# Dilated heads interleaved with matrix tiles, and the layer embedding's projection placed after the output projection

## The reference

```python
# second block, in outline
h  = rmsnorm(x, g_mix) @ w_in          # 6 parts of 512 columns: b, c, x for the convolution; q, k, v
conv = b * causal_dwconv3(c * x)       # 512 wide
att  = dilated_attention(rmsnorm(q), rmsnorm(k), v)    # 8 heads of 64, causal, additive distance bias
x = x + concat(rmsnorm(conv), rmsnorm(att)) @ w_out
x = x + (silu(causal_dwconv3(rmsnorm(x) @ w_gate)) * (rmsnorm(x) @ w_up)) @ w_down     # 2816 wide
out = x + sigmoid(rmsnorm(x) @ w_ple_gate) * (p @ w_ple_proj)   # p: layer embedding, 512 x 256
```

## Time and profile before

| | us |
|---|---|
| median of 3 runs (lowest, highest) | 1833.47 (1832.82, 1835.03) |
| the profiled execution | 1833.88 |
| its span in the profile | 1832.0 |
| TensorE busy | 1790.5 |
| VectorE busy | 985.4 |
| ScalarE busy | 667.1 |
| GpSimd busy | 1.9 |

### The profile page before, as it was taken

How to read it: one execution, slowest core, us unless ns; L and a number is a source line. 1 busy time by engine, 2 the same in 40 slices (tenths; PEclk the granted TensorE clock), 3 DMA queues, 4 the chain that set the end, 5 groups by cost and what they waited for, 6 DMA issues and landing times.

```text
span 1832.0 us, 23458 instructions
## 1 busy us (share of the span) xinstructions
PE 1790.5 (98%) x9636; PEld 1527.6 (83%) x9636; DVE 985.4 (54%) x1423; ACT 667.1 (36%) x935; POOL 1.9 (0%) x11
## 2 busy tenths in 40 slices
PE   9999999999999999999999999989999999999998
PEld 7777998888889988988888889878878788888886
DVE  3666753434347576743434357646457665256554
ACT  3455441313133666432322236225344322122332
POOL 0000000000000000000000000000000000000000
PEclk9999999999999999999999999988889999999999
DMA  7220232232223112222222231210202223322341
GB/s 280 93 69 29 94 109 98 87 114 92 92 92 111 63 59 78 85 92 81 103 92 93 90 115 70 92 69 11 82 24 104 92 92 115 138 92 92 115 147 60
DMA packets 28596, 169.73 MB, mean 93 GB/s; under 512 B 2848, under 2 KB 7392, under 8 KB 9440
## 3 DMA queue, kind: packets, MB, share of 16 engines
q1 hardware_dynamic: 22592, 156.44, 23.9%
q10 hardware_dynamic: 5920, 12.08, 2.0%
HBM read 166.39 MB, written 5.27 MB: 94 GB/s over the span
## 4 chain that ended last, share of the span: by engine, by line
PE 89%; DVE 5%; ACT 3%; DMA 1%; issue 1%; DVEq 0%; SPq 0%; ACTq 0%
PE ps L1546 29%; PE ps L1548 28%; PE ps L1547 28%; PE ps L1679 2%; DVE w_lo L840 1%; ACT w_hi L407 1%; DMA stage<-slabs 1%; PE ps L1658 1%; PE ps L1892 0%; PE ps L1619 0%; ACT y L564 0%; PE ps L2024 0%; ACT act_hi L569 0%; PE ps L2034 0%; PE ps L1799 0%
## 5 line engine op out<-in xcount | busy, mean ns | idle before, releaser
L1546 PE MATMUL ps<-act_hi,w_lo 128*128 128x512 f32 (+1 forms) x1504 | 544.3, 362 | 8.1 <-DVE act_lo L840 2.6
L1548 PE MATMUL ps<-act_lo,w_hi 128*128 128x512 f32 (+1 forms) x1504 | 538.5, 358 | 0.0
L1547 PE MATMUL ps<-act_hi,w_hi 128*128 128x512 f32 (+1 forms) x1504 | 538.3, 358 | 0.0
L407 ACT ACTIVATE w_hi<-stage 128x2048 fp32r<-128x2048 f32 (+4 forms) x147 | 267.5, 1820 | 390.8 <-PE ps L1548 389.5
L840 DVE TENSOR_TENSOR w_lo<-stage,w_hi 128x2048 fp32r<-128x2048 f32 (+6 forms) x152 | 322.5, 2123 | 93.4 <-ACT w_hi L407 86.4
L1546 PEld LDWEIGHTS ps<-act_hi,w_lo 128*128 128x128 f32 x1504 | 284.2, 189 | 54.0 <-issue 5.9
L1548 PEld LDWEIGHTS ps<-act_lo,w_hi 128*128 128x128 f32 x1504 | 283.9, 189 | 42.0
L1547 PEld LDWEIGHTS ps<-act_hi,w_hi 128*128 128x128 f32 x1504 | 283.9, 189 | 40.2
L1546 PE MATMUL ps<-hid_hi,w_lo 128*128 128x512 f32 (+1 forms) x608 | 218.5, 359 | 2.1 <-DVE w_lo L840 2.1
L1548 PE MATMUL ps<-hid_lo,w_hi 128*128 128x512 f32 (+1 forms) x608 | 216.9, 357 | 0.0
L1547 PE MATMUL ps<-hid_hi,w_hi 128*128 128x512 f32 (+1 forms) x608 | 215.4, 354 | 0.0
(11 more groups left out here) (288 smaller groups left out, 2217.6 us busy)
## 6 DMA issues: line engine op xcount, KB each, us to landing
stage<-slabs SPq DMA_DIRECT2D x147, 1024.0 KB, 4.8
bias_rows<-bias_line ACTq DMA_DIRECT2D x1, 3072.0 KB, 16.3
strips<-dilated ACTq DMA_DIRECT2D x2, 1024.0 KB, 4.9
out<-y ACTq DMA_DIRECT2D x4, 512.0 KB, 2.6
y<-x_t ACTq DMA_DIRECT2D x3, 512.0 KB, 8.9
strips<-bias_rows ACTq DMA_DIRECT2D x1, 1024.0 KB, 5.3
strips<-bias_rows ACTq DMA_DIRECT2D x2, 512.0 KB, 3.9
stage<-slabs SPq DMA_DIRECT2D x3, 256.0 KB, 8.6
```

What stands on the lines that cost most here:

```text
L407: nc.scalar.activation(w_hi[p][:, 0:w], stage[s][:, 0:w], ACT.Copy).then_inc(cast_hi, 1)
L1546: mm(out, l_lo, r_hi, start=start, stop=False, skip_group_check=shared)
L1547: mm(out, l_hi, r_hi, start=False, stop=False, skip_group_check=shared)
L1548: return mm(out, l_hi, r_lo, start=False, stop=stop, skip_group_check=shared)
```

## The change

Both versions have 148 slabs and the same matmul products; their places differ.

- The three slabs of the convolution's second half (`CONV_B`) stand behind the first half's q, k and v. Their six tiles of 24 matmuls go one at a time into bank 7 (`conv_steps`, `conv_tile`), between the parts of heads 0 to 3.
- The output projection is packed by rows: two slabs for the convolution's half (`MIX_OUT`), whose eight tiles of 12 matmuls go into bank 7 between the parts of heads 4 to 7 (`mix_tile`), and two for the attention's half (`MIX_ATT`, `att_steps`).
- All heads mix into bank 6, where they had alternated between 6 and 7.
- `PLE_PROJ` comes after `MIX_ATT` and before `FFN_A`, in five parts (`PROJ_PARTS`). ScalarE copies the result to `proj`, where it stays to the end. `p_lo` is made by GpSimd.
- In the convolution, c times x carries the factor twice: c is scaled by `rstd2`, which ScalarE makes as the square of `rstd`, and x is multiplied with it straight from PSUM, which saves one VectorE instruction. A one-column copy behind each read now gives the signal.

```diff
-DIL_HALF = 95
+DIL_A = 92
+CONV_B = 95
+DIL_B = 98
 MIX_OUT = 101
-FFN_A, FFN_A_DOWN = 105, 117
+MIX_ATT = 103
+PLE_PROJ = 105
+FFN_A, FFN_A_DOWN = 106, 118
+FFN_B, FFN_B_DOWN = 126, 136
...
...
+        def att_bank(t):
+            return (0, 1, 2, 7, 3, 4, 5, 6)[t]
...
+            pool.wait_ge(p_split, 1)
+            nc.gpsimd.tensor_tensor(p_lo[:, :, :], p_raw[:, :, :], p_hi[:, :, :].bitcast(F32), ALU.subtract)\
+                .then_inc(p_split, 1)
+            pool.wait_ge(p_split, 2)
...
-                for j in range(3):
...
             root("attn")
-            rstd_copy("attn", stat, 2)
+            rstd_copy("attn", stat, 6)
             for j in range(4):
-                rms_out(MIX_OUT + j, [2 * j, 2 * j + 1], j, "g_ffn")
-                cast(MIX_OUT + j + 2)
-            act.wait_ge(slab_read, FFN_A)
-            act.dma_start(p_raw[:, :, :], ple_t).then_inc(p_landed, 16)
+                g = MIX_ATT + j // 2
+                rms_out(*((slab_read, g + 1) if j % 2 else (part_read, 10 + j // 2)), [2 * j, 2 * j + 1], j, "g_ffn")
+                if j % 2:
+                    cast(g + 2)
+                if j == 0:
+                    act.wait_ge(p_landed, 16)
+                    nc.scalar.activation(p_hi[:, :, :], p_raw[:, :, :], ACT.Copy).then_inc(p_split, 1)
+            for n, (t, m) in enumerate(PROJ_PARTS):
+                b = att_bank(t)
+                if n < 4:
+                    act.wait_ge(proj_done, n + 1)
+                    nc.scalar.activation(proj[:, t:t + m, :], ps[:, b:b + m, :], ACT.Copy).then_inc(proj_read, 1)
+                else:
+                    act.wait_ge(slab_done, PLE_PROJ + 1)
+                    nc.scalar.activation(proj[:, t:t + m, :], ps[:, b:b + m, :], ACT.Copy).then_inc(slab_read, 1)
...
+            def conv_tile(j):
+                k = j % 2
+                if k:
+                    dve.wait_ge(slab_done, CONV_B + j // 2 + 1)
+                else:
+                    dve.wait_ge(part_done, j // 2 + 1)
+                dst, by = ((zc[:, k, :], rstd2[:, :]), (u_pad[:, k, 2:T + 2], zc[:, k, :]),
+                           (yc[:, 2 + k, :], rstd[:, :]))[j // 2]
+                ins = nc.vector.tensor_tensor(dst, ps[:, 7, :], by, ALU.mult)
+                if k:
+                    ins.then_inc(slab_read, 1)
+                    dve.wait_ge(slab_read, CONV_B + j // 2 + 1)
+                else:
+                    ins.then_inc(part_read, 1)
+                    dve.wait_ge(part_read, j // 2 + 1)
...
+                    dve.wait_ge(slab_done, MIX_OUT + j // 4 + 1)
+                    .then_inc(slab_read if j % 4 == 3 else part_read, 1)
+            dve.wait_ge(slab_read, DIL_A)
...
+            conv_tile(0)
+            dil_bias(0)
+            divide(dil, d_prob, 0)
+            conv_tile(1)
+            for u in range(4):
+                if u < 3:
+                    dil_bias(u + 1)
+                if u == 1:
+                    conv_taps(1, 0)
+                elif u == 2:
+                    conv_taps(1, 1)
+                elif u == 3:
+                    link(nc.vector.tensor_tensor(yc[:, 2, :], yc[:, 2, :], conv[:, 0, :], ALU.mult))
+                if u < 3:
+                    divide(dil, d_prob, u + 1)
+                if u:
+                    dil_out(u - 1)
+                turn_lo(dil, d_pt_hi, d_pt_lo, u)
+                conv_tile(2 + u)
+                if u == 0:
+                    cast(CONV_B + 2)
+                elif u == 2:
+                    cast(DIL_B)
...
+            dve.wait_ge(dil.turned, 3 * 4)
+            qk_out(1, 1)
...
+            dil_bias(4)
+            mix_tile(0)
+            divide(dil, d_prob, 4)
+            mix_tile(1)
+            for u in range(4, 8):
+                if u < 7:
+                    dil_bias(u + 1)
+                    mix_tile(2 * (u - 3))
+                    divide(dil, d_prob, u + 1)
+                if u > 4:
+                    dil_out(u - 1)
+                turn_lo(dil, d_pt_hi, d_pt_lo, u)
+                if u < 7:
+                    mix_tile(2 * (u - 3) + 1)
+                if u == 4:
+                    cast(MIX_OUT + 1)
...
-                g = MIX_OUT + j
-                b = banks(g)
-                dve.wait_ge(slab_done, g + 1)
-                link(nc.vector.tensor_tensor(conv[:, :, :], ps[:, 4 + b:6 + b, :], pair(stat[:, :]), ALU.mult))
-                link(nc.vector.tensor_tensor(y[:, 2 * j:2 * j + 2, :], y[:, 2 * j:2 * j + 2, :], conv[:, :, :],
-                                             ALU.add))
-                nc.vector.tensor_tensor(y[:, 2 * j:2 * j + 2, :], y[:, 2 * j:2 * j + 2, :], ps[:, b:b + 2, :],
-                                        ALU.add).then_inc(slab_read, 1)
+                g = MIX_ATT + j // 2
+                if j % 2:
+                    dve.wait_ge(slab_done, g + 1)
+                else:
+                    dve.wait_ge(part_done, 10 + j // 2)
+                if j == 1:
+                    nc.vector.tensor_tensor(mix_part[:, 0, :], ps[:, att_bank(2), :], stat[:, :], ALU.mult)
+                    link(nc.vector.tensor_tensor(mix_part[:, 1, :], ps[:, att_bank(3), :], stat[:, :], ALU.mult))
+                else:
+                    b = att_bank(2 * j)
+                    link(nc.vector.tensor_tensor(mix_part[:, :, :], ps[:, b:b + 2, :], pair(stat[:, :]), ALU.mult))
+                nc.vector.tensor_tensor(y[:, 2 * j:2 * j + 2, :], y[:, 2 * j:2 * j + 2, :], mix_part[:, :, :],
+                                        ALU.add).then_inc(slab_read if j % 2 else part_read, 1)
                 rms_out([2 * j, 2 * j + 1], j, "g_ffn", SQUARED["ffn"])
-                cast(g + 2)
+                if j % 2:
+                    cast(g + 2)
+            cast(PLE_PROJ + 2)
             mean_squares("ffn", 7, 1.0)
...
-                if u % 4 >= 2:
-                    pe.wait_ge(dil.out_read, u - 1)
-                mix(dil, u, 6 + u % 2, d_pt_hi, d_pt_lo, dil_values)
...
+            def conv_steps(j, steps):
+                g, m = CONV_B + j // 2, j % 2
+                if 0 in steps:
+                    if j == 0:
+                        pe.wait_ge(qk_full, 2)
+                    elif j % 2:
+                        pe.wait_ge(part_read, j // 2 + 1)
...
+                        pe.wait_ge(slab_read, g)
+                    pe.wait_ge(cast_lo, g + 1)
+                for k in steps:
+                    c = (k * 2 + m) * P
+                    last = product(ps[:, 7, :], w_hi[place(g)][:, c:c + P], w_lo[place(g)][:, c:c + P],
+                                   act_hi[:, k, :], act_lo[:, k, :], k == 0, k == KT - 1)
+                if 7 in steps:
+                    last.then_inc(slab_done if m else part_done, 1)
...
+            g = DIL_A
+            plain(g)
+            plain(g + 1, ready=between({3: lambda: head_sums(0, 4), 6: lambda: head_spread("q0", 4)}))
+            values(g + 2, between({1: lambda: k_sums(0), 2: lambda: head_spread("k0", 6)}))
+            conv_steps(0, range(8))
+            pe.wait_ge(slab_read, g + 3)
+            pe.wait_ge(dil_ready, 2)
+            score(dil, 0, dil_operands, 0)
+            conv_steps(1, range(8))
+            pe.wait_ge(dil_ready, 3)
+            for u in range(3):
+                score(dil, u + 1, dil_operands, 0)
+                conv_steps(2 + u, range(4))
+                if u:
+                    dil_mix(u - 1)
+                turn(dil, u, d_prob)
+                conv_steps(2 + u, range(4, 8))
+            dil_mix(2)
+            turn(dil, 3, d_prob)
+            conv_steps(5, range(8))
+            dil_mix(3)
+            g = DIL_B
+            pe.wait_ge(dil.biased, 16)
+            plain(g, ready=between({6: conv_sums}))
...
+            plain(g + 1, ready=between({1: lambda: spread("conv", 7).then_inc(spread_done, 1),
+                                        3: lambda: head_sums(2, 4), 6: lambda: head_spread("q1", 4)}))
+            values(g + 2, between({1: lambda: k_sums(1), 2: lambda: head_spread("k1", 6)}))
+            pe.wait_ge(slab_read, g + 3)
+            pe.wait_ge(dil_ready, 3 + 2)
+            score(dil, 4, dil_operands, 4)
...
+                    dil_mix(u - 1)
+                turn(dil, u, d_prob)
+                mix_tile(2 * (u - 3) + 1)
+            dil_mix(6)
+            turn(dil, 7, d_prob)
             pe.wait_ge(dil.biased, 4 * 8)
-            for j in range(4):
-                g = MIX_OUT + j
-                s, b = place(g), banks(g)
-                if j >= 2:
-                    pe.wait_ge(slab_read, g - 1)
-                if j == 1:
-                    pe.wait_ge(rstd_ready, RSTD["attn"])
-                pe.wait_ge(cast_lo, g + 1)
-                for k in range(KT):
-                    if j == 0 and k == 1:
-                        dil_turn(7)
-                    if j == 0 and k == 4:
-                        dil_mix(7)
-                        pe.wait_ge(dil.turn_lo, 3 * 8)
-                    if j == 0:
```

(36 more changed lines are left out.)

533 lines of the change are left out of this document (279 added, 254 removed).

## The result

The changed kernel takes 1816.14 us (median of four runs, 1815.55 to 1817.42) against 1833.14 for the kernel before beside it; the ratio is 0.9907, 95% interval 0.989 to 0.9924. Forecast were 1819 and 1811 to 1829. The profiled executions took 1815.94 and 1833.88 us: 17.9 us apart, where the forecast's sum had 14.7.

A forecast was written before the change was run, and what follows sets the result against it. TensorE was taken to bound the kernel, busy 1790.5 of 1832.0 us. Losses of 42.1 us before (14.2 idle, 27.6 clock, 0.3) less 27.4 after gave a gain of 14.7, so 1819 us, range 1811 to 1829.

The forecast's parts named there:

- The heads: Woven heads: TensorE waits of 2.5 us left in the first half and 5.8 in the second.
- The unnamed 1.0 us: First half's heads: one more us of wait for what laying out the engines' orders misses, inside the 2.5.
- those at mixes 6 and 7: Second half's heads: 0.8 us of waits at these mixes and the attention sums, inside the 5.8.
- The bank as a toll: Rival: every bank 7 tile waits for VectorE's read, 11.8 us more, 1831, or half of that, 1825; 18%.
- its counter-argument: Against the toll on bank 7: a score of 2.1 us stands between most tiles.
- The clock term: Clock losses: 1.3 us at q and k, 2.5 behind the second half's first score, 1.5 after projection waits; 5.3 together.
- The projection: Output projection and PLE_PROJ: TensorE waits 5.0 us for PLE_PROJ's cast, then 4.7 for ScalarE's copies; loss 9.7.
- S: The time at which the factor `stat` is ready, ahead of the four pairs of the output projection.
- GpSimd: 1.2 us: At the pairs: GpSimd's `p_lo` holds up VectorE for its length, 0 to 1.2 us, taken as 1.2.
- FFN_B: Without PLE_PROJ as cover, the second down slab there waits: 2.0 us lost, bounds 1 and 3.
- The start: ScalarE's square into `rstd2` and a one-column copy behind each read: 0.9 us later, between 0 and 1.2.
- (1 - c) x L: Most that a mean clock c costs over a stretch of length L, with TensorE always ready; 27.6 us before the change.

The follow-up runs named there:

- changed_again: The changed kernel run once more without any change, to see its spread: 1817.58 us, ratio 0.9912 to the kernel before.

## Why the prediction was right, and where its sizes were off

- **The heads: right, and better.** Neither half has a wait over 1.4 us. The first half has 1.2 us of waits (0.45 and 0.76, forecast 2.5), the second 4.5 (0.24, 0.91, 1.39, 0.78, 0.98, 0.23, forecast 5.8); each is a wait that the prediction named. The unnamed 1.0 us and those at mixes 6 and 7 did not come.
- **The bank as a toll** is a real price, 0.8 us a tile, and hidden by what stands between, as its counter-argument said.
- **The clock term was mis-sized and misplaced.** Forecast 5.3 us with 2.5 behind the first score; the profiled execution had 3.1, all behind the projection's wait. The fall behind the first score is real in others (1.7 to 3.4 us). The prediction counted as certain what comes in a part of the executions. Its price of 2.5 us for a fall was read too low as well: the stretch at 0.94 begins inside the fall, which costs 3.2 us in full (0.52 from 1357.5 to 1364.2 us of the kernel before).
- **The projection.** The first wait was 5.5 us (forecast 5.0, and GpSimd's 1.2 beside it), the second 1.5 (4.7). The chain took 31.5 us from S, as forecast (31). The projection filled part of the second wait by running 6.2 us at half clock: clock and wait are one loss here, not two. Together 7.0 + 3.1 = 10.1, with GpSimd's part inside, against 9.7 + 1.5 of clock + 1.2 = 12.4.
- **GpSimd: 1.2 us, as forecast,** shown by the row that goes from 2.43 to 1.23 us when `p_lo` runs elsewhere. The Trainium skill (SBUF — State Buffer, "Who interferes with whom") has the two block each other, and the trace agrees (2.43 us for 1.23). The Trainium skill (GPSIMD Engine Reference, "Performance versus the Vector engine") has GpSimd at 1.96 times VectorE's time; by that estimate the instruction would take 2.4 us, and it took 2.40. The loss was half of that; VectorE's sum began 1.05 us after it. That the forecast 1.2 was met is in part luck: it was an upper bound taken from VectorE's own instruction, and the overlap that made it so was not worked out.
- **FFN_B: 1.8 us** (forecast 2.0).
- **The start:** a wait of 1.82 us for 1.08, 0.7 later (forecast 0.9).
- **The sum was wrong on the other side as well.** The terms after are 0.7 + 1.2 + 4.5 + 3.1 + 7.0 + 1.8 = 18.3 us, not 27.4, and by the 42.1 of before the gain would be 23.8. It was 17.9. Of the 5.9 us between, 2.2 are the idle time of before, counted again in (1 - c) x L (6.9 x 0.11 + 1.4 x 0.24 + 1.6 x 0.04 + 4.3 x 0.24). 2.7 are a cost without a term, good to about 1 us because the clocks are rounded to 0.01: 1157.7 to 1392.0 us without its losses is 218.5 us, the like of before 204.9 + 10.9 for the projection. It lies in the pieces, as these starts on TensorE show, beside the earlier trace rows (score, half a tile, transposes, half a tile, score):

```profile
1213.25 0.32 PE L1666 MATMUL ps<-dk_hi,dq_lo 64*128 64x128 f32 x1
...
1215.37 0.50 PE L1666 MATMUL ps<-act_hi,w_lo 128*128 128x512 f32 x1
...
1218.25 1.25 PE L1799 MATMUL ps<-mat,d_prob 128*128 128x128 f32 x10
1219.25 0.48 PE L1666 MATMUL ps<-act_hi,w_lo 128*128 128x512 f32 x1
...
1222.20 0.33 PE L1666 MATMUL ps<-dk_hi,dq_lo 64*128 64x128 f32 x1
```

  Twelve matmuls take 2.88 and 2.95 us where dense ones take 12 x 0.227 = 2.72; the weave has sixteen such pieces. 0.6 us more stand ahead of the whole stretch (GpSimd's `u_pad` at 1109.5 for 1108.8); that is spread between executions and no cost of the change, since the same step stands at 1108.4 in `changed_again`. 0.4 us stay unexplained. So the forecast was close in part by luck, because errors of 9 and 6 us cancelled in part.
- **What the prediction did not see** is that the two parts of the change work against each other: the weave wins 23 us and the move lost 5 to 7. It set the move's cost of 9.7 + 1.2 + 2.0 against a cover of 0.3 us, but never asked what the pairs would cost without it.

Open: what decides whether the clock falls. The profiled executions give only how often: behind the wait of 1.82 us in 7 of 13, behind that of 1.39 us in 3 of 9, and behind that of 1.3 us at the second down slab of FFN_B in 4 of 10.

## What to carry to other kernels

Putting independent tiles into a chain through several engines pays twice, in idle time and in the clock. Find the price of the pieces in it, about 0.2 us a switch here. When work is moved in front of a slow chain, add up the chain's engine, not TensorE's wait: removing that wait alone gave nothing, shortening the chain alone 1.4 us, both together, with ScalarE's copies in the gaps, hid it wholly. Compare two places for a step only when each has its best order around it.
